# Differential attention on one core: the next key tile's steps moved between a head's score groups, and three of its four rows turned at the head's end

## The chip, the cores and the metric

The kernel runs on one core of one Trainium2 chip. The time is the device time of one execution in microseconds (us), the median of three executions. Five engines run their own instruction streams and meet through semaphores: TensorE (PE in the profile, its weight loads PEld), VectorE (DVE), ScalarE (ACT), GpSimd (POOL) and SyncE (SP, which only issues the loads).

## What is computed

A small transformer of two blocks, 512 positions of width 1024, in float32. The change is in one part of the second block, the differential attention, with 8 heads of two maps of 64 each:

```
k, v   = split(rms_norm(x, g_kv) @ w_kv)
q      = (h @ w_q), 8 heads x 2 maps x 64
logits = einsum('bqhmd,bkhmd->bhmqk', q, k) * 64**-0.5 + bias[h, dist]     (causal)
probs  = softmax(logits)
attn   = probs[:, :, 0] - lam * probs[:, :, 1]
o      = rms_norm(attn @ v, subln_g) * (1 - lambda_init)
mix    = o @ w_o
```

## The kernel before

Every tensor lies with its features (or keys) on the 128 partitions and the 512 positions along the free dimension. Every float32 product is made of three matmuls: each operand is split into a rounded high part (made by ACT, `..._hi`) and the rest (made by DVE or POOL, `..._lo`), and high x high, high x low and low x high are summed in a PSUM bank (`mm`, L755). Weights come in units of 8 blocks of 128x128: SP loads a unit (L715), ACT writes its high part (L732, tile WH), DVE its low part (L741, tile WL), always two units ahead.

There is no scheduler. Each engine's order is written out by hand in a function of its own (`pe_dif`, `act_dif`, `dve_dif`, `pool_dif`), all with the same loop over the heads h = 0..7, and a wait is put in where an event of another engine is needed. `plan_dif` lists in program order who sits in which PSUM bank and which temporary tile; a step that writes a bank waits until the bank's previous tenant has been read (`freed`, L384).

In a head, PE does these steps:

- **scores(h, i)** for the four rows of 128 queries, i = 0..3 (L2269): per map p three matmuls of 128*(i+1) keys into a bank of its own. The banks come from a ring of three (banks 2 to 4). DVE then adds the bias and finds the row maximum (L2544), ACT takes the exponential (L2411), and after two rows DVE's `combine` (L2554 to L2564) subtracts the two maps.
- **turn(h, i)** (L2282): the i+1 blocks of a row are transposed into a bank of a ring of two (banks 5 and 6; rows 0 and 1 share one). ACT copies the high part (L2418), DVE writes the low part (L2570), which frees the bank.
- **key(h + 1)** (L2252): the next head's key tile, eight steps k = 0..7 of three 512-column matmuls, read out by DVE at L2525.
- **value** (L2256): one half of a value tile, 48 matmuls of 256 columns, read out at L817 (ACT) and L826 (DVE).
- **values(h - 1)** (L2291): the product of the turned rows with v, in bank 7.
- **sums_of(h - 1)** (L2304) and **finish(h - 2)** (L2314): the sum of squares of a head's output (which DVE turns into an inverse root, L2583 and L880 to L892), and the spread of that root over the partitions, which ACT copies (L2434) and DVE multiplies in (L2596).

Key tiles, value halves, sums and spreads share a ring of two banks (0 and 1). The seats are handed out in the order of `plan_dif`; before, the key tile is seated ahead of the spread:

```
if h < 7:
    key(h + 1)
...
if h >= 2:
    finish(h - 2)
```

so a key tile follows a value half in its bank, and the spread follows the sums. `sums_of(h - 1)` stands at the end of head h on PE, and DVE reads its bank in the next head, after `scores`.

In head 7 there is no next key tile; steps of the output projection `w_o_2` (k, m) stand there instead, by the table `DIF_OUT`, in which each name is a place in the head and each pair is one step of three 512-column matmuls.

Of the kernel before, what the change touches and what calls it, by code (L numbers as in the profile page):

```python
# [48 lines left out]
def nope_q(h):  # L49
# [49 lines left out]


DIF_OUT = {
    "head 7, a": [(k, 0) for k in range(5)],
    "head 7, b": [(5, 0)],
    "turn": [(k, m) for k in range(3) for m in (1, 2, 3)],
    "values": [(k, m) for k in (3, 4) for m in (1, 2, 3)],
    "sums": [(5, 1), (5, 2)],
    "root": [(5, 3)] + [(6, m) for m in range(4)],
    "spread": [(k, 4) for k in range(7)],
# [163 lines left out]
class Net:  # L272
# [352 lines left out]
    def plan_dif(self):  # L625
        seat, bank = self.seat, self.bank
        self.ring = Ring(bank[0:6])
        self.plan_entry("dif")
        seat(self.tmp.next(), "t", "dif", "lam")
        seat(bank[7], "dif", "q", 6)  # L630
        seat(bank[6], "dif", "q", 7)
        pr, srg, ptr = Ring(bank[0:2]), Ring(bank[2:5]), Ring(bank[5:7])
        self.extra = [Slot(self.fd(4096, 512)), Slot(self.fd(4608, 512)), Slot(self.R2), Slot(self.acc[:, :])]
        own, self.tmp = self.tmp, Ring(self.tmps + self.extra)
        tmp = self.tmp

        def key(h):
            seat(pr.next(), "dif", "k", h)
            seat(tmp.next(), "t", "dif", "k", h)

        def value(c, p):
            seat(pr.next(), "dif", "v", c, p)

        def scores(h, i):
            for p in range(2):
                seat(srg.next(), "dif", "s", h, i, p)
                if p == 0 or i >= 2:
                    seat(tmp.next(), *self.dif_row(h, i, p))

        def turn(h, i):  # L650
            seat(ptr.next(), "dif", "t", h, i)

        def values(h):
            seat(bank[7], "dif", "pv", h)
            seat(tmp.next(), "t", "dif", "osq", "h", h)

        def sums_of(h):
            seat(pr.next(), "dif", "hs", h)

        def finish(h):  # L660
            seat(pr.next(), "dif", "hr", h)
            for x in "rt":
                seat(tmp.next(), "t", "dif", x, h)

        for h in range(8):
            seat(tmp.next(), "t", "dif", "q", h)
        key(0)
        value(0, 0)
        for h in range(8):
            scores(h, 0)  # L670
            if h:
                turn(h - 1, 2)
            scores(h, 1)
            scores(h, 2)
            if h:
                turn(h - 1, 3)
            if h < 7:
                key(h + 1)
            else:
                seat(bank[1], "dif", "o", 0)  # L680
                pr = Ring(bank[0:1])
            if h >= 2:
                finish(h - 2)
            scores(h, 3)
            if h:
                values(h - 1)
            if h < 7:
                value((h + 1) // 2, (h + 1) % 2)
            turn(h, 1)
            if h:  # L690
                sums_of(h - 1)
        turn(7, 2)
        turn(7, 3)
        finish(6)
        values(7)
        sums_of(7)
        finish(7)
        for m in range(1, 5):
            seat(bank[m + 1], "dif", "o", m)
        self.tmp = own  # L700
        for m in range(5, 8):
            seat(bank[m - 5], "dif", "o", m)
        for m in range(1, 8):
            seat(own.next(), "t", "dif", "osq", m)
# [1543 lines left out]
    def pe_dif(self, pe):  # L2248
        QZ, pt, xin = self.dif_qz, self.dif_pt, self.xin(0)

        def key(h):
            self.pe_tile(pe, ("dif", "k", h), "w_kv_2", h, KD, xin, (lambda k: ("xkv", k)) if h == 0 else None,  # L2252
                         {4: lambda: finish(h - 3)} if h >= 3 else None)

        def value(c, halves):
            self.pe_natural(pe, "dif", c, "w_kv_2", (8 + 2 * c, 9 + 2 * c), KD, xin, None, halves)  # L2256
# [17 lines left out]
        def turn(h, i):  # L2274
            b = self.dif_turned(h, i)
            pe.wait_ge(*self.at("probs", "dif", h, i))
            if i != 1:
                for w in self.freed("dif", "t", h, max(i, 1)):
                    pe.wait_ge(*w)
            for j in range(i + 1):  # L2280
                sl = slice(128 * j, 128 * j + 128)
                m = pe.transpose(b[:, sl], self.dif_s(h, i, 0)[:, sl], self.ident[:, :])  # L2282
            m.then_inc(*self.tick("pe_turn", ("pe", "dif", "t", h, i), ("free", *self.dif_row(h, i, 0))))
# [24 lines left out]
        def finish(h):  # L2308
            b, y = self.place["dif", "hr", h], self.small(("hy", h), 4)
            pe.wait_ge(*self.at("hy", h))  # L2310
            for w in self.freed("dif", "hr", h):
                pe.wait_ge(*w)
            for c in range(4):
                m = pe.matmul(b[:, 128 * c:128 * c + 128], y[:, c:c + 1].broadcast_to([P, P]), self.ident[:, :],  # L2314
                              start=True, stop=True)
            m.then_inc(*self.tick("pe_spread", ("pe", "dif", "hr", h)))
# [26 lines left out]
        for h in range(8):  # L2343
            scores(h, 0)
            if h:
                turn(h - 1, 2)
            scores(h, 1)
            scores(h, 2)
            if h:
                turn(h - 1, 3)  # L2350
            if h < 7:
                key(h + 1)
            else:
                out(DIF_OUT["head 7, a"])
                finish(5)
            scores(h, 3)
            if h:
                values(h - 1)
            if h < 7:
                value((h + 1) // 2, [(h + 1) % 2])  # L2360
            else:
                out(DIF_OUT["head 7, b"])
            turn(h, 0)
            turn(h, 1)
            if h:
                sums_of(h - 1)
        turn(7, 2)
        out(DIF_OUT["turn"])
        turn(7, 3)
        finish(6)  # L2370
        out(DIF_OUT["values"])
# [10 lines left out]
    def act_dif(self, act):  # L2382
# [79 lines left out]
        for h in range(8):  # L2462
            scores(h, 0)
            if h:
                turn(h - 1, 2)
            scores(h, 1)
            scores(h, 2)
            if h:
                turn(h - 1, 3)
            if h < 7:  # L2470
                key(h + 1)
            else:
                out(DIF_OUT["head 7, a"])
                finish(5)
                rounded(5)
            scores(h, 3)
            if h:
                values(h - 1)
            if h < 7:
                c = (h + 1) // 2  # L2480
                if h % 2:
                    self.hi_to(act, BLOCK["w_kv_2", KD - 1, 9 + 2 * c])
                value(c, [(h + 1) % 2])
                if h % 2 == 0:
                    self.hi_to(act, BLOCK["w_kv_2", KD - 1, h + 1])
            else:
                out(DIF_OUT["head 7, b"])
            turn(h, 0)
            turn(h, 1)
        turn(7, 2)  # L2490
        out(DIF_OUT["turn"])
        turn(7, 3)
        finish(6)
        out(DIF_OUT["values"])
# [9 lines left out]
    def dve_dif(self, dve):  # L2504
# [9 lines left out]
                *self.tick("q_in", ("q_in", h), ("free", *b)))  # L2514

        def key(h):
            if h % 2 == 0:
                self.lo_to(dve, BLOCK["w_kv_2", KD - 1, h])
            if h >= 3:
                finish(h - 3)  # L2520
            t, b = ("t", "dif", "k", h), ("dif", "k", h)
            dve.wait_ge(*self.at("pe", *b))
            for w in self.freed(*t):
                dve.wait_ge(*w)
            dve.tensor_tensor(self.place[t], self.place[b], R, ALU.mult).then_inc(  # L2525
                *self.tick("dif_kin", ("dif_kin", h), ("free", *b)))
# [106 lines left out]
        for h in range(8):  # L2633
            scores(h, 0)
            if h:
                turn(h - 1, 2)
            scores(h, 1)
            scores(h, 2)
            if h:
                turn(h - 1, 3)  # L2640
            if h >= 2:
                sums_of(h - 2)
            combine(h, 0)
            if h < 7:
                key(h + 1)
            else:
                out(DIF_OUT["head 7, a"])
                finish(5)
            scores(h, 3)
            combine(h, 2)  # L2650
            floor_of(h)
            if h < 7:
                c = (h + 1) // 2
                if h % 2:
                    self.lo_to(dve, BLOCK["w_kv_2", KD - 1, 9 + 2 * c])
                value(c, [(h + 1) % 2])
                if h % 2 == 0:
                    self.lo_to(dve, BLOCK["w_kv_2", KD - 1, h + 1])
            else:
                out(DIF_OUT["head 7, b"])  # L2660
            turn(h, 0)
            turn(h, 1)
        turn(7, 2)
        sums_of(6)
        out(DIF_OUT["turn"])
        turn(7, 3)
        finish(6)
        out(DIF_OUT["values"])
# [286 lines left out]
```

## Time and profile before

| | us |
|---|---|
| median of 3 executions | 2221.17 |
| lowest and highest | 2210.81, 2221.62 |
| the profiled execution, its own time | 2223.64 |
| its span, first to last instruction | 2221.8 |
| PE busy in it | 2032.3 (91%) |
| DVE, ACT, POOL busy | 1246.1, 814.0, 379.0 |
| mean granted TensorE clock | 0.947 of full speed |
| matmuls of the score groups (L2269), first to last start | 1512.9 to 1691.7 |

The part that the change touches is the stretch from about 1513 to 1745 us of the span, a tenth of it. The rest of the kernel is the same in both. In what follows M is the moment at which PE ends the value half of a head, the last long matmul run before the next head's first scores; times in head h are counted from the M that ends head h-1. The stretches of the windows below run from M to M, heads 0 to 6 in order, and the last from head 7's M to its values(6).

### The profile page before, as it was taken

The numbers are of one execution on the slowest core, as the hardware profiler recorded it, in microseconds if no ns is written. First come the engines' busy times: TensorE is split into PE (matmuls) and PEld (weight loads), VectorE is DVE, ScalarE is ACT, GpSimd is POOL, SyncE is SP. The second block draws the span as 40 slices with busy tenths as digits, with TensorE's granted clock in tenths as the row PEclk, the third lists the DMA queues.
The fourth block names the chain that finished last, engine by engine and source line by source line (L and its number), as shares of the span: only waits on it lengthen the run. The fifth ranks groups of instructions, "written<-read, shape, count | busy, mean of one in ns | idle before, by whom it ended". The sixth has DMA issues, their size and how long they took to land.

```text
span 2221.8 us, 25395 instructions
## 1 busy us (share of the span) xinstructions
PE 2032.3 (91%) x9756; PEld 1696.6 (76%) x9756; DVE 1246.1 (56%) x2013; ACT 814.0 (37%) x1307; POOL 379.0 (17%) x300
## 2 busy tenths in 40 slices
PE   7999999989788999999999998798889899999996
PEld 6888888767667777877888787676777778887875
DVE  6665664266665354457777425565555577774255
ACT  4233232243333332334444223334444444442232
POOL 3322321110222210121111011121001311110111
PEclk9999999989888999999999999798889999999997
DMA  4222222312101123322223332122111122232221
GB/s 166 81 81 86 79 83 86 96 57 86 38 29 37 61 97 103 113 67 86 95 95 105 104 96 68 54 84 81 57 39 49 66 85 95 95 105 104 96 68 46
DMA packets 53664, 178.91 MB, mean 81 GB/s; under 512 B 6151, under 2 KB 8711, under 8 KB 53544
## 3 DMA queue, kind: packets, MB, share of 16 engines
q1 hardware_dynamic: 53544, 177.29, 24.0%
q8 instruction: 78, 1.28, 0.2%
q14 instruction: 42, 0.34, 0.1%
HBM read 172.55 MB, written 4.72 MB: 80 GB/s over the span
## 4 chain that ended last, share of the span: by engine, by line
PE 59%; DVE 11%; ACT 4%; issue 3%; POOL 1%; DVEq 0%; ACTq 0%
PE pb L758 55%; DVE WL L741 2%; ACT WH L732 1%; DVE X L922 1%; PE pb L2269 1%; PE pb L855 1%; DVE T L1703 1%; PE pb L839 1%; DVE FR L956 1%; PE pb L1457 1%; ACT T L942 1%; DVE sm L1692 0%; PE pb L1889 0%; DVE T L916 0%; DVE FR L826 0%
## 5 line engine op out<-in xcount | busy, mean ns | idle before, releaser
L758 PE MATMUL pb<-FR,WH 128*128 128x512 f32 x4552 | 1457.6, 402 | 70.5 <-DVE FR L956 28.7
L758 PEld LDWEIGHTS pb<-FR,WH 128*128 128x128 f32 x4552 | 874.2, 194 | 266.5 <-issue 39.6
L758 PE MATMUL pb<-FR,WL 128*128 128x512 f32 x2276 | 906.8, 398 | 0.0
L741 DVE TENSOR_TENSOR WL<-stage,WH 128x1024 fp32r<-128x1024 f32 x311 | 408.7, 1333 | 517.3 <-ACT WH L732 516.3
L758 PEld LDWEIGHTS pb<-FR,WL 128*128 128x128 f32 x2276 | 441.4, 194 | 95.9
L732 ACT ACTIVATE WH<-stage 128x1024 fp32r<-128x1024 f32 x311 | 319.2, 1051 | 122.0 <-PE pb L758 109.1
L758 PE MATMUL pb<-WH,FR 128*128 128x256 f32 x832 | 154.7, 284 | 6.0 <-DVE T L1675 3.8
L758 PE MATMUL pb<-FR 128*128 128x256 f32 (+3 forms) x752 | 129.1, 325 | 13.5 <-DVE T L1265 12.2
L758 PEld LDWEIGHTS pb<-FR 128*128 128x128 f32 x752 | 117.6, 204 | 27.6 <-DVE T L1265 14.8
L758 PEld LDWEIGHTS pb<-WH,FR 128*128 128x128 f32 x832 | 131.4, 192 | 8.0 <-DVE T L1675 4.7
L948 POOL TENSOR_TENSOR acc<-acc,T 128x512 f32<-128x512 f32 x56 | 75.7, 1352 | 277.1 <-ACT T L942 276.6
L1040 POOL TENSOR_TENSOR acc<-acc,T 128x512 f32<-128x512 f32 x48 | 62.1, 1294 | 349.2 <-ACT T L1023 296.3
L758 PE MATMUL pb<-WL,FR 128*128 128x256 f32 x416 | 117.7, 283 | 0.0
L931 ACT ACTIVATE FR<-X,cols 128x512 fp32r<-128x512 f32 x64 | 45.4, 721 | 148.2 <-DVE X L922 148.2
L758 PEld LDWEIGHTS pb<-WL,FR 128*128 128x128 f32 x416 | 79.8, 192 | 0.1
L2101 POOL TENSOR_TENSOR FR<-FD,FR 128x512 fp32r<-128x512 f32 x26 | 34.2, 1316 | 242.2 <-ACT FR L2032 242.2
L1023 ACT ACTIVATE T<-pb 128x512 f32<-128x512 f32 x42 | 25.8, 614 | 126.7 <-PE pb L758 126.7
L1869 ACT ACTIVATE FD<-FD,cols 128x512 f32<-128x512 f32 x42 | 30.2, 724 | 101.5 <-DVE FD L2062 57.5
L922 DVE TENSOR_TENSOR X<-X,T 128x512 f32<-128x512 f32 x64 | 58.9, 922 | 0.2
L1357 POOL TENSOR_TENSOR FR<-T,FR 128x512 fp32r<-128x512 f32 (+3 forms) x32 | 28.0, 906 | 167.6 <-ACT FR L1193 167.6
L916 DVE SCALAR_TENSOR_TENSOR T<-FD,cols,pb 128x512 f32<-128x512 f32 x64 | 47.2, 738 | 14.6 <-PE pb L855 14.6
L817 ACT ACTIVATE FR<-pb,held 128x256 fp32r<-128x256 f32 x64 | 26.4, 474 | 76.3 <-PE pb L758 76.3
(223 smaller groups left out, 1669.7 us busy)
## 6 DMA issues: line engine op xcount, KB each, us to landing
stage<-in_ws SPq DMA_DIRECT2D x311, 512.0 KB, 3.5
X<-in_xT SPq DMA_DIRECT2D x8, 256.0 KB, 5.9
FD<-in_decay SPq DMA_DIRECT2D x8, 256.0 KB, 3.7
FD<-scr SPq DMA_DIRECT2D x1, 2048.0 KB, 10.0
out_dram<-X SPq DMA_DIRECT2D x8, 256.0 KB, 2.0
scr<-T SPq DMA_DIRECT2D x8, 160.0 KB, 1.8
scr<-FD SPq DMA_DIRECT2D x8, 160.0 KB, 1.9
FD<-in_rope_b SPq DMA_DIRECT2D x2, 512.0 KB, 3.4
```

The source lines that it names most:

```text
L732: act.activation(hi, src, ACT.Copy).then_inc(*self.tick("w_hi", ("w_hi", u)))
L741: dve.tensor_tensor(lo, src, hi.bitcast(F32), ALU.subtract).then_inc(*self.tick("w_lo", ("w_lo", u)))
L758: m = pe.matmul(out, l, r, start=first and i == 0, stop=last and i == n - 1)
L817: act.activation(dst(t)[0], src, ACT.Copy, scale=self.hold(y)[:, t:t + 1]).then_inc(*self.tick("v_hi", ("v_hi", s, h, t)))
L916: dve.scalar_tensor_tensor(out=t, in0=self.Y[k], scalar=self.col(name, base + k), in1=self.place["spread", s, "post"], op0=ALU.mult, op1=A ...
L922: dve.tensor_tensor(self.xt(k), self.xt(k), self.place["t", s, "z", k], ALU.add).then_inc(*self.tick("added", ("x", s, k), ("free", "t", s ...
L931: act.activation(self.xin(at)(0, k), self.xt(k), ACT.Copy, scale=self.col(name, base + k)).then_inc(*self.tick("xg_hi", ("xg_hi", s, g, k)))
L948: pool.tensor_tensor(self.acc[:, :], self.acc[:, :], self.place["t", s, "sq", k], ALU.add).then_inc(*self.tick("acc", ("acc", s, "x", k), ...
L1040: pool.tensor_tensor(self.acc[:, :], self.acc[:, :], self.place["t", s, "osq", m], ALU.add).then_inc(*self.tick("acc", ("acc", s, "y", m), ...
L1357: pool.tensor_tensor(S[:, 1280 + o:1280 + o + n], self.place["t", "ret", "s", h, j][:, 0:n], S[:, o:o + n].bitcast(F32), ALU.subtract).the ...
L1869: act.activation(self.place[o], self.place[u], ACT.Copy, scale=w).then_inc(*self.tick("tap", done))
L2101: pool.tensor_tensor(M[:, (NF + m) * 512:(NF + m) * 512 + 512], self.place[t], M[:, 512 * m:512 * m + 512].bitcast(F32), ALU.subtract).the ...
```

## The change

In a head, PE's steps were: scores 0, turn(h-1, 2), scores 1, scores 2, turn(h-1, 3), the key tile with the spread in it, scores 3, values, the value half, turn 0, turn 1, sums. Now they are: scores 0, turn(h-1, 3), key steps 0 and 1, scores 1, key steps 2 to 4, scores 2, key step 5, the spread, key steps 6 and 7, scores 3, values, the value half, turn 0, turn 1, turn 2, sums. ACT and DVE follow in their streams; DVE does the arithmetic of `sums_of(h - 2)` now between its row 3 and the bias of scores 1. `plan_dif` seats the spread ahead of the key tile. In head 7 the table spreads the first output steps over the same gaps. Cut to what matters:

```diff
 DIF_OUT = {
-    "head 7, a": [(k, 0) for k in range(5)],
-    "head 7, b": [(5, 0)],
+    "head 7, a": [(0, 0), (1, 0)],
+    "head 7, b": [(2, 0), (3, 0)],
...
@@ plan_dif
         for h in range(8):
             scores(h, 0)
             if h:
-                turn(h - 1, 2)
+                turn(h - 1, 3)
             scores(h, 1)
             scores(h, 2)
-            if h:
-                turn(h - 1, 3)
-            if h < 7:
-                key(h + 1)
-            else:
+            if h == 7:
                 seat(bank[1], "dif", "o", 0)
                 pr = Ring(bank[0:1])
             if h >= 2:
                 finish(h - 2)
+            if h < 7:
+                key(h + 1)
             scores(h, 3)
...
             turn(h, 1)
+            turn(h, 2)
             if h:
                 sums_of(h - 1)
-        turn(7, 2)
         turn(7, 3)
@@ pe_dif
         def key(h):
             self.pe_tile(pe, ("dif", "k", h), "w_kv_2", h, KD, xin, (lambda k: ("xkv", k)) if h == 0 else None,
-                         {4: lambda: finish(h - 3)} if h >= 3 else None)
+                         h and {1: lambda: scores(h - 1, 1), 4: lambda: scores(h - 1, 2),
+                                5: lambda: h >= 3 and finish(h - 3)})
...
             scores(h, 0)
             if h:
-                turn(h - 1, 2)
-            scores(h, 1)
-            scores(h, 2)
-            if h:
                 turn(h - 1, 3)
             if h < 7:
                 key(h + 1)
             else:
                 out(DIF_OUT["head 7, a"])
+                scores(h, 1)
+                out(DIF_OUT["head 7, b"])
+                scores(h, 2)
+                out(DIF_OUT["head 7, c"])
                 finish(5)
...
             turn(h, 0)
             turn(h, 1)
+            if h < 7:
+                turn(h, 2)
             if h:
                 sums_of(h - 1)
+        out(DIF_OUT["turn"])
         turn(7, 2)
-        out(DIF_OUT["turn"])
         turn(7, 3)
@@ act_dif
             if h:
-                turn(h - 1, 2)
+                turn(h - 1, 3)
             scores(h, 1)
             scores(h, 2)
-            if h:
-                turn(h - 1, 3)
...
             turn(h, 1)
+            if h < 7:
+                turn(h, 2)
@@ dve_dif
         def key(h):
+            if h >= 3:
+                finish(h - 3)
             if h % 2 == 0:
                 self.lo_to(dve, BLOCK["w_kv_2", KD - 1, h])
-            if h >= 3:
-                finish(h - 3)
...
             scores(h, 0)
             if h:
-                turn(h - 1, 2)
-            scores(h, 1)
-            scores(h, 2)
-            if h:
                 turn(h - 1, 3)
             if h >= 2:
                 sums_of(h - 2)
+            scores(h, 1)
             combine(h, 0)
+            scores(h, 2)
             if h < 7:
                 key(h + 1)
...
             turn(h, 1)
+            if h < 7:
+                turn(h, 2)
```

How this stands in the instruction streams, in head 4. First PE, from scores 0 (128 columns) on, before; FD and T are the tiles of the rows 2 and 3 that are turned (L2282):

```order
L2269 MATMUL pb<-FR 128x128 [waits s_biased,s_k_lo,s_q_lo]
L2269 MATMUL pb<-FR 128x128 x5
L2282 MATMUL pb<-ident,FD 128x128 [waits s_pt_lo,s_probs]
L2282 MATMUL pb<-ident,FD 128x128 x2
L2269 MATMUL pb<-FR 128x256 [waits s_biased]
L2269 MATMUL pb<-FR 128x256 x5
L2269 MATMUL pb<-FR 128x384 [waits s_biased]
L2269 MATMUL pb<-FR 128x384 x5
L2282 MATMUL pb<-ident,T 128x128 [waits s_pt_lo,s_probs]
L2282 MATMUL pb<-ident,T 128x128 x3
L758 MATMUL pb<-FR,WH 128x512 [waits s_w_lo,s_v_lo]
L758 MATMUL pb<-FR,WH 128x512
```

And in the changed kernel (the same lines are one number higher here), where FD has gone to the end of the head before:

```order
L2270 MATMUL pb<-FR 128x128 [waits s_biased,s_k_lo,s_q_lo]
L2270 MATMUL pb<-FR 128x128 x5
L2283 MATMUL pb<-ident,T 128x128 [waits s_pt_lo,s_probs]
L2283 MATMUL pb<-ident,T 128x128 x3
L758 MATMUL pb<-FR,WH 128x512 [waits s_w_lo,s_o_var]
L758 MATMUL pb<-FR,WH 128x512
L758 MATMUL pb<-FR,WL 128x512
L758 MATMUL pb<-FR,WH 128x512 x2
L758 MATMUL pb<-FR,WL 128x512
L2270 MATMUL pb<-FR 128x256 [waits s_biased]
L2270 MATMUL pb<-FR 128x256 x5
L758 MATMUL pb<-FR,WH 128x512 x2
```

The groups of 256 and 384 columns, scores 1 and 2, now have two and three key steps ahead of them; the first key matmul waited on `s_v_lo` (the value half's bank) and now waits on `s_o_var`, which DVE's first instruction of `sums_of` gives.

DVE in the same head before, from its row 2 (128x3x128) to `sums_of(2)` (the two groups between are the biases of scores 1 and 2):

```order
L2570 TENSOR_TENSOR FR<-pb,FR 128x3x128 [waits s_pt_hi]
L2544 ISA T,sm<-pb,FD 128x256 [waits s_pe_turn,s_pe_scores]
L2544 ISA sm 128x1
L2544 ISA T,sm<-pb,FD 128x256 [waits s_pe_scores]
L2544 ISA sm 128x1
L2544 ISA FD,sm<-pb,FD 128x384 [waits s_pe_turn,s_pe_scores]
L2544 ISA sm 128x1
L2544 ISA FD,sm<-pb,FD 128x384 [waits s_probs,s_pe_scores]
L2544 ISA sm 128x1
L2570 TENSOR_TENSOR FR<-pb,FR 128x4x128 [waits s_pt_hi]
L2583 SCALAR_TENSOR_TENSOR sm<-pb,sm 128x4 [waits s_pe_sums,s_o_var]
```

And in the changed kernel, from the end of the bias of scores 0:

```order
L2546 ISA T,sm<-pb,FD 128x128 [waits s_pe_scores]
L2546 ISA sm 128x1
L2572 TENSOR_TENSOR FR<-pb,FR 128x4x128 [waits s_pt_hi]
L2585 SCALAR_TENSOR_TENSOR sm<-pb,sm 128x4 [waits s_pe_sums,s_o_var]
L880 TENSOR_SCALAR sm<-sm 128x4 [waits s_o_var]
L882 SCALAR_TENSOR_TENSOR sm<-sm 128x4 [waits s_newton]
L884 TENSOR_TENSOR sm<-sm 128x4 [waits s_newton]
L886 SCALAR_TENSOR_TENSOR sm<-sm 128x4 [waits s_newton]
L889 SCALAR_TENSOR_TENSOR sm<-sm 128x4 [waits s_newton] x2
L892 SCALAR_TENSOR_TENSOR sm<-sm 128x4 [waits s_newton]
L2546 ISA T,sm<-pb,FD 128x256 [waits s_pe_turn,s_pe_scores]
L2546 ISA sm 128x1
```

Row 3 and the sums stand ahead of the bias of scores 1 now, and row 2 has gone ahead of the bias of scores 0.

## Rows read from the trace of the kernel before

**Rows 1.** The waits of PE, 1480 to 1725 us: in total, times, longest.
```profile
PE pb L2269 <- DVE sm L2544: 24.3, 16, 2.7
```
**Rows 2.** M to M: length, busy PE, PEld, DVE, ACT, POOL; clock, DMA share, GB/s.
```profile
1512.96:1531.12 18.16, 15.92 (x98) 13.28 (x99) 8.13 (x29) 6.27 (x19) 1.30 (x1) 0.91 0.17 59
1531.12:1556.03 24.91, 20.43 (x122) 17.06 (x120) 14.22 (x36) 11.86 (x29) 1.30 (x1) 0.86 0.16 49
1556.03:1579.53 23.50, 20.84 (x136) 17.68 (x135) 11.56 (x41) 9.26 (x26) 2.58 (x2) 0.93 0.10 39
1579.53:1605.01 25.48, 21.79 (x137) 18.60 (x135) 16.19 (x45) 13.08 (x30) 2.60 (x2) 0.87 0.17 47
1605.01:1629.14 24.13, 21.72 (x137) 18.60 (x136) 11.56 (x41) 9.33 (x27) 2.60 (x2) 0.86 0.10 39
1629.14:1653.93 24.79, 21.47 (x136) 18.20 (x134) 16.10 (x45) 13.02 (x30) 2.54 (x2) 0.86 0.15 52
1653.93:1677.19 23.26, 20.86 (x136) 17.94 (x135) 11.57 (x41) 9.29 (x26) 2.59 (x2) 0.93 0.09 36
1677.19:1693.02 15.83, 11.51 (x66) 8.83 (x64) 10.23 (x34) 8.03 (x22) 0.00 (x0) 0.78 0.09 33
```
**Rows 3.** Timeline of PE, head 3 (M = 1579.53): start, duration, idle before, releaser.
```profile
1583.50 0.63 PE L2269 MATMUL pb<-FR 64*128 64x256 f32 x6 [1.89 <-DVE sm L2544]
1585.93 1.33 PE L2269 MATMUL pb<-FR 64*128 64x384 f32 x6 [1.80 <-DVE sm L2544]
1587.19 1.11 PE L2282 MATMUL pb<-ident,T 128*128 128x128 f32 x4
1587.95 1.20 PE L758 MATMUL pb<-FR,WH 128*128 128x512 f32 x2
...
1591.73 0.63 PE L758 MATMUL pb<-FR,WH 128*128 128x512 f32 x2
...
1592.43 0.62 PE L758 MATMUL pb<-FR,WH 128*128 128x512 f32 x2
```
**Rows 4.** Timeline of DVE, head 3, from its share of the value half on.
```profile
1580.44 0.88 DVE L826 SCALAR_TENSOR_TENSOR FR<-pb,held,FR 128x256 fp32r<-128x256 f32 x2 [4.06 <-ACT FR L817]
1581.39 1.22 DVE L741 TENSOR_TENSOR WL<-stage,WH 128x1024 fp32r<-128x1024 f32 x1
1582.53 0.61 DVE L2570 TENSOR_TENSOR FR<-pb,FR 128x128 fp32r<-128x128 f32 x2
1583.06 0.28 DVE L2544 CUSTOM_DVE_ANT_0 T<-pb,FD 128x128 f32<-128x128 f32 x1
...
1584.88 0.56 DVE L2570 TENSOR_TENSOR FR<-pb,FR 128x384 fp32r<-128x384 f32 x1 [1.32 <-ACT FR L2418]
...
1590.16 0.69 DVE L2570 TENSOR_TENSOR FR<-pb,FR 128x512 fp32r<-128x512 f32 x1 [1.86 <-ACT FR L2418]
1590.77 0.15 DVE L2583 SCALAR_TENSOR_TENSOR sm<-pb,sm 128x4 f32<-128x4 f32 x1
...
1601.07 0.74 DVE L2564 SCALAR_TENSOR_TENSOR T<-T,sm 128x512 f32<-128x512 f32 x1
```
**Rows 5.** Timeline of ACT, head 3: the exponential of row 0, the copies of rows 2 and 3.
```profile
1583.60 0.40 ACT L2411 ACTIVATE T<-T,sm 128x128 f32<-128x128 f32 x1 [1.80 <-DVE sm L2544]
...
1584.38 0.47 ACT L2418 ACTIVATE FR<-pb 128x384 fp32r<-128x384 f32 x1
...
1589.55 0.57 ACT L2418 ACTIVATE FR<-pb 128x512 fp32r<-128x512 f32 x1
```
**Rows 6.** Timeline of DVE, head 4 (M = 1605.01), rows 0 and 1.
```profile
1606.71 0.61 DVE L2570 TENSOR_TENSOR FR<-pb,FR 128x128 fp32r<-128x128 f32 x2
```
**Rows 7.** Timeline of PE, head 0: the two waits.
```profile
1515.09 0.62 PE L2269 MATMUL pb<-FR 64*128 64x256 f32 x6 [1.66 <-DVE sm L2544]
1516.29 1.26 PE L2269 MATMUL pb<-FR 64*128 64x384 f32 x6 [0.58 <-DVE sm L2544]
```
**Rows 8.** Timeline of PE, head 7: values(6).
```profile
1693.02 2.10 PE L758 MATMUL pb<-FR 128*128 128x512 f32 x12 [0.95 <-DVE acc L2596]
```

More of the change, by code:

```diff
@@ L101 @@
 DIF_OUT = {
-    "head 7, a": [(k, 0) for k in range(5)],
-    "head 7, b": [(5, 0)],
-    "turn": [(k, m) for k in range(3) for m in (1, 2, 3)],
-    "values": [(k, m) for k in (3, 4) for m in (1, 2, 3)],
+    "head 7, a": [(0, 0), (1, 0)],
+    "head 7, b": [(2, 0), (3, 0)],
+    "head 7, c": [(4, 0)],
+    "head 7, d": [(5, 0)],
+    "turn": [(k, m) for k in range(2) for m in (1, 2, 3)],
+    "values": [(k, m) for k in (2, 3, 4) for m in (1, 2, 3)],
     "sums": [(5, 1), (5, 2)],
@@ L2361, in pe_dif @@
             else:
-                out(DIF_OUT["head 7, b"])
+                out(DIF_OUT["head 7, d"])
             turn(h, 0)
             turn(h, 1)
+            if h < 7:
+                turn(h, 2)
             if h:
                 sums_of(h - 1)
+        out(DIF_OUT["turn"])
         turn(7, 2)
-        out(DIF_OUT["turn"])
         turn(7, 3)
@@ L2472, in act_dif @@
             else:
-                out(DIF_OUT["head 7, a"])
+                out(DIF_OUT["head 7, c"])
                 finish(5)
@@ L2486, in act_dif @@
             else:
-                out(DIF_OUT["head 7, b"])
+                out(DIF_OUT["turn"])
             turn(h, 0)
             turn(h, 1)
+            if h < 7:
+                turn(h, 2)
         turn(7, 2)
-        out(DIF_OUT["turn"])
         turn(7, 3)
@@ L2646, in dve_dif @@
             else:
-                out(DIF_OUT["head 7, a"])
+                out(DIF_OUT["head 7, c"])
                 finish(5)
@@ L2659, in dve_dif @@
             else:
-                out(DIF_OUT["head 7, b"])
+                out(DIF_OUT["turn"])
             turn(h, 0)
             turn(h, 1)
+            if h < 7:
+                turn(h, 2)
+        sums_of(6)
         turn(7, 2)
-        sums_of(6)
-        out(DIF_OUT["turn"])
         turn(7, 3)
```

## The prediction

> **What bounds the kernel there.** PE is busy 91% of the span, so the first question is where it is not. I read the waits of PE over the attention first [rows 1]: the score groups wait for DVE 16 times, 24.3 us in all, twice in each head. Then the windows from M to M [rows 2]: a head takes 23.3 to 25.5 us, PE is busy 20.4 to 21.8 of them, and the granted clock is 0.86 to 0.93 of full speed; in heads 3 and 5 DVE has one more weight unit to make than in heads 2, 4 and 6, and they are the long ones. Then the timelines of one head. PE waits 1.89 us before scores 1 and 1.80 before scores 2 [rows 3], because the ring of score banks is three deep and DVE frees a bank only with the bias. DVE in turn is late because it has the value half, a weight unit and the turned rows in front of that bias [rows 4], and between them it waits for ACT's copies [rows 5]. Behind the waits the clock is at its low level: three key steps take from 1587.95 to 1591.73, 1.26 each, and the next one 0.70 [rows 3].
>
> So the attention costs more than its work in two ways, waits and the clock that falls behind them. The change means to put key steps into the two gaps. No arithmetic is added or taken away; what counts is which wait ends last in the new order.
>
> **The new start of a head, heads 2 to 6.** PE now does turn 2 at the end of the head before, so after scores 0 it comes to turn(h-1, 3) at about M + 2.1 (in head 3 before, the idle of 1.89 that ends at 1583.50 began at M + 2.1, after the same work) [rows 3]. Two waits follow.
>
> First, row 3 goes into the bank that rows 0 and 1 of the same head sit in, and that is free when DVE has written their low parts. In head 4 that is 1606.71 + 0.61, M + 2.3 [rows 6]; in head 3, with the weight unit ahead, 1582.53 + 0.61, M + 3.6 [rows 4]. With 0.1 for the semaphore PE goes on at M + 2.4 or M + 3.7, after 0.3 or 1.6 idle. The four blocks take 0.76 at the low clock [rows 3], 0.4 at the full one.
>
> Second, the key tile. Since the spread is now seated ahead of it, its bank's previous tenant is the sums of head h-2, which DVE reads with its first instruction of `sums_of`, and that stands behind the low part of row 3. The chain in an even head: DVE does row 2 (0.48, from 1584.88 to the next start) up to M + 2.75, and the bias of scores 0 (0.54 until ACT starts) [rows 4, 5], so ACT starts at M + 3.3; its exponentials take 0.78 (1583.60 to 1584.38), and only then comes its copy of row 3, 0.57 [rows 5], to M + 4.7; DVE's low part takes 0.61 and the read of the sums 0.15 [rows 4], to M + 5.45. PE starts the key tile at M + 5.55, after 2.7 idle. In heads 3 and 5 everything is 1.3 later, M + 6.85. Before, PE stood idle for 2.4 and 3.7 in these two kinds of head; now for 3.0 and 4.3. The gaps that the change fills are replaced by one that is larger.
>
> Behind it nothing else should wait: scores 1 needs the bias of scores 0, done before; scores 2 comes 2.1 us of key steps later, DVE's bias of scores 1 needs about 0.7 after its matmuls; scores 3 has three key steps and the spread ahead of it.
>
> The work from the start of the key tile to the next M was 17.06 in head 3 (1587.95 to 1605.01), of which the three slow steps were 3.78 where full clock gives 2.1, so 15.4 [rows 2, 3]. Scores 1 (0.6) and scores 2 (half of 1.33) come into it: 16.7 [rows 3]. Then the clock. Before, from the end of the second wait the rest of a head is scores 2, row 3 and the 15.4, 16.5; the wait ends at M + 5.1 or 6.4, which gives 21.6 and 22.9, and heads 2 to 6 took 23.50, 25.48, 24.13, 24.79 and 23.26 [rows 2]. The differences, 1.9, 2.6, 2.5, 1.9 and 1.7, are the low clock, 2.1 on average. The idle stretch is no shorter now, so I take 2.1 again. One more term in heads 3 and 5: ACT has a weight unit ahead of its copy of the spread there (its busy time is 13.1 in them against 9.3 [rows 2]), the spread itself comes later in the key tile, and values(h-1) needs the bank that DVE frees with that product. In head 7, also an odd one, this wait was 0.95 [rows 8]; I take 0.65, between nothing and that.
>
> An even head: 5.55 + 16.7 + 2.1 = 24.35. Heads 3 and 5: 6.85 + 16.7 + 2.1 + 0.65 = 26.3. Three and two of them make 125.65, against 121.16 before (1556.03 to 1677.19) [rows 2]: **+4.5**.
>
> **Head 1** has no sums of an older head, so its key tile can start behind row 3. It is one of the heads with a weight unit: row 3 at M + 3.7, key tile at M + 4.1, then 16.7 less the spread it doesn't have (eight blocks of 128 columns, 0.9 by the four of a row), plus 2.1: 22.0 against 24.91 [rows 2]: **-2.9**.
>
> **Head 0** turns nothing at its start. Its waits were 1.66 and 0.58 [rows 7]; two key steps (1.4) cover the first but for about 0.3, so 1.9 goes, and without the idle time the clock should stay: 0.09 of 18.16, 1.6 [rows 2]. **-3.5**.
>
> **Head 7.** Its output steps wait for no sums bank, but DVE now has row 3 and the eight small operations of the sums ahead of the bias of scores 1, and scores 2 waits for that; and values(6), which waited 0.95 before [rows 8], hangs on the same chain of ACT and DVE. I cost it at **0**, between -1 and +1. The output steps behind it are 42 as before, in another order; PE has nothing but them to wait with, and they cover the turns of rows 2 and 3 by six steps of 0.7 instead of nine.
>
> **Moved for nothing.** Turn 2 at the head's end needs `combine` of rows 2 and 3. Before, in head 3, DVE's product for row 2 stood just before that of row 3, which ended at 1601.07 + 0.74, 3.2 us ahead of M [rows 4]; in odd heads it will come about 2 us later. The cover is values and the value half, some 8 us of PE (the 15.4 less eight key steps, the spread and scores 3); if it is gone, each us late is one us of PE. The unit loads of SP are not moved past anything.
>
> **The sum** is 4.5 - 2.9 - 3.5 + 0 = -1.9. The profiled execution took 2223.64, which gives 2221.7; it lies 2.5 above the median of the runs, 2221.17, and so the median to expect is **2219**. A measurement of this kernel can tell about 0.5%, 11 us, from no change; its three runs alone spread over 10.8.
>
> The Trainium skill (Perfetto Trace Analysis, Optimization Strategy) says that the same gap repeating on the engine that should be saturated can mean too few banks for the next tile. The trace agrees: both old waits and both new ones are for a bank. Taken strictly it speaks against this change, which adds no bank: the 24.3 us would then only change their place, and the result would be 2221. The same page (Matmul Optimizations) says that TensorE scales its power with use and that matmuls should go out back to back in batches; by it a key tile cut into three pieces would lose a little, while here the pieces stand back to back with the scores.
>
> **Rivals.**
> *The gaps are covered (8%).* If the key tile's bank were free in time, all 24.3 us would go [rows 1] and with them the low clock behind, 2.1 in five heads and about 6.5 in heads 0, 1 and 7: 41 us, **2180**. For it speaks that 1.4 and 2.1 us of key steps match gaps of 1.9 and 1.8; against it the wait on `s_o_var` at the first key matmul.
> *The waits stay, but the clock does not fall (16%).* The idle time comes in one piece behind short work, and the key tile then runs without a break. If the clock stays up in heads 1 to 6, 2.1 us less in each: **2206**. Against it: before, it fell in every head, also in head 4 with 2.4 us idle [rows 2].
> *Slower (16%).* Turn 2 at the end of the head comes to the path. Its place is the last 0.3 us of a head: DVE's product for row 2 hangs on the spread, the weight unit and the key tile's readout ahead of the bias of scores 3. Once that chain is over about 2 us later than I walked it, PE stands there idle, the clock falls a second time, and the next head starts later on all engines. At 1.5 us of wait and 1.3 of clock in five heads that is 14 us: **2233**. Against it speaks the slack of 3.2 us before [rows 4].
> *The forecast (60%)*: the waits change places and heads 0 and 1 pay for heads 2 to 6, **2219**, and with the ends of its terms 2210 to 2228 (a clock loss of 1.0 to 3.2 per head, somewhat wider than the 1.7 to 2.6 seen, is 6 us each way over six heads, head 7 one, the 0.65 one, rounding one).
>
> **How the numbers follow.** The range runs from below the clock case to just under the slower case, 2203 to 2232; outside lie the covered case (8%) and part of the slower one. Faster by over 0.5% (below 2210) holds the first two rivals, 0.24; slower (above 2232) the third, 0.16; within is 0.60.
>
> **What the next profile should show.** The waits of score groups for DVE near nothing in heads 1 to 6 instead of 24.3; a new wait of the key tile's first matmul for the sums (L2583, now L2585), five times, about 2.7 each; waits of row 3's turn for the low part (L2570, now L2572), 0.3 and 1.6; heads 2 to 6 of 24.3 and 26.3 us, heads 0 and 1 shorter by 3 each. The forecast is wrong if the key tile starts before M + 4.5 in head 4, if the clock stays at 1.00 there, or if PE waits at the end of a head.

## The result, and the profile after

The changed kernel takes 2227.36 us, median of 19 executions (2224.45 to 2229.72), against 2223.02 us for the kernel before in as many (2210.81 to 2227.47). The ratio is 1.0021, 95% interval 1.0012 to 1.003: slower by 0.2%. That lies within the 0.5% that the prediction called no change and inside its range, but the forecast was 1.9 us down, and the median went 4.3 up. The profiled executions have spans, first to last instruction, of 2223.1 after and 2221.8 before.

The waits of PE over the attention in the changed kernel (engine, tile, line, who was waited for; us in total, times, longest):

```profile
PE pb L758 <- DVE sm L2585: 11.7, 5, 2.4
PE pb L2283 <- DVE FR L2572: 10.1, 7, 2.6
PE pb L758 <- DVE acc L2598: 5.2, 3, 3.7
...
PE pb L2270 <- DVE sm L2546: 1.3, 2, 0.7
```

The score groups' 24.3 us [rows 1] are down to 1.3, and two new waits make 21.8: the key tile's first matmul for the read of the sums (L2585), and row 3's turn for the low part of rows 0 and 1 (L2572). A third one, of values(h-1) for the spread's product (L2598), has grown from 0.9 to 5.2.

The windows from M to M in the changed kernel: heads 0 to 6, head 7 up to values(6), then to the end of the output matmuls, then to the first addition of the next stage (length, busy PE, PEld, DVE, ACT, POOL; clock, DMA share, GB/s):

```profile
1510.94:1525.77 14.83, 14.76 (x98) 12.03 (x99) 8.13 (x29) 6.28 (x19) 1.30 (x1) 1.00 0.22 72
1525.77:1546.07 20.30, 17.68 (x121) 14.65 (x119) 12.67 (x35) 11.85 (x28) 1.30 (x1) 1.00 0.17 52
1546.07:1570.49 24.42, 21.18 (x137) 17.52 (x135) 12.65 (x43) 9.13 (x26) 2.55 (x2) 0.93 0.14 44
1570.49:1597.47 26.98, 22.08 (x136) 18.15 (x135) 15.52 (x45) 12.95 (x30) 2.84 (x2) 0.87 0.12 40
1597.47:1621.54 24.07, 21.19 (x137) 17.53 (x135) 11.95 (x42) 9.13 (x26) 2.56 (x2) 0.93 0.12 44
1621.54:1648.59 27.05, 22.15 (x137) 18.23 (x135) 15.53 (x45) 12.96 (x30) 2.84 (x2) 0.87 0.12 40
1648.59:1672.65 24.06, 21.18 (x136) 17.43 (x135) 11.95 (x42) 9.14 (x26) 2.54 (x2) 0.93 0.12 44
1672.65:1689.12 16.47, 9.61 (x65) 7.28 (x64) 10.27 (x34) 7.90 (x22) 0.00 (x0) 0.98 0.08 33
1689.12:1741.92 52.80, 52.03 (x244) 43.83 (x244) 18.14 (x38) 20.96 (x36) 12.12 (x9) 0.94 0.22 75
1741.92:1748.81 6.89, 3.86 (x25) 3.39 (x23) 2.05 (x10) 1.08 (x2) 0.00 (x0) 0.82 0.10 39
```

The last two stretches in the kernel before:

```profile
1693.02:1743.21 50.19, 49.41 (x243) 41.41 (x244) 18.08 (x38) 20.91 (x36) 12.15 (x9) 1.00 0.25 79
1743.21:1749.40 6.19, 3.16 (x25) 2.79 (x23) 2.06 (x10) 1.08 (x2) 0.00 (x0) 0.93 0.13 52
```

Set beside [rows 2]: head 0 is 3.3 us shorter, head 1 4.6, heads 2 to 6 are 5.4 longer (126.58 against 121.16), head 7 up to values(6) 0.6 longer. Up to that point the changed kernel is 1.9 us ahead. Then it loses 2.6 in the output matmuls, at a clock of 0.94 where it was 1.00, and 0.7 in the norm behind. The whole attention, from the first M to that addition, takes 237.87 against 236.44: 1.4 us more.

PE in head 4 of the changed kernel (M = 1597.47; start, duration, idle before and who ended it):

```profile
1598.85 0.55 PE L2270 MATMUL pb<-FR 64*128 64x128 f32 x6
1599.94 0.63 PE L2283 MATMUL pb<-ident,T 128*128 128x128 f32 x4 [0.54 <-DVE FR L2572]
1602.91 1.13 PE L758 MATMUL pb<-FR,WH 128*128 128x512 f32 x2 [2.35 <-DVE sm L2585]
1605.68 0.95 PE L2270 MATMUL pb<-FR 64*128 64x256 f32 x6
```

And DVE at the same place:

```profile
1600.17 0.28 DVE L2546 CUSTOM_DVE_ANT_0 T<-pb,FD 128x128 f32<-128x128 f32 x1
...
1602.10 0.69 DVE L2572 TENSOR_TENSOR FR<-pb,FR 128x512 fp32r<-128x512 f32 x1 [1.43 <-ACT FR L2421]
1602.70 0.15 DVE L2585 SCALAR_TENSOR_TENSOR sm<-pb,sm 128x4 f32<-128x4 f32 x1
```

PE starts row 3 at M + 2.47 and the key tile at M + 5.44. DVE stands idle for 1.43 us, waiting for ACT's copy of row 3, while the small operation that PE waits for is ready to run and stands behind it.

In head 7 (M = 1672.65) the long wait is at values(6). ACT, DVE and PE in the changed kernel:

```profile
1686.02 1.04 ACT L732 ACTIVATE WH<-stage 128x1024 fp32r<-128x1024 f32 x1
1686.96 0.57 ACT L2437 ACTIVATE R<-pb 128x512 f32<-128x512 f32 x1
...
1687.09 1.22 DVE L741 TENSOR_TENSOR WL<-stage,WH 128x1024 fp32r<-128x1024 f32 x1 [2.32 <-ACT WH L732]
1688.23 0.74 DVE L2598 SCALAR_TENSOR_TENSOR acc<-pb,keep,R 128x512 f32<-128x512 f32 x1
...
1684.44 0.96 PE L2270 MATMUL pb<-FR 64*128 64x512 f32 x6 [0.61 <-DVE sm L2546]
1689.12 3.75 PE L758 MATMUL pb<-FR 128*128 128x512 f32 x12 [3.72 <-DVE acc L2598]
```

The copy and the product of the spread stand behind a weight unit on both engines. PE waits 3.72 us, against 0.95 before [rows 8], and its twelve matmul records behind the wait take 3.75 us instead of 2.10. The wait is longer for two reasons: PE gets there 2.1 us earlier in the head (M + 12.75, before M + 14.88), and the product comes 0.6 later. It comes later although its spread comes earlier from PE, because ACT reaches row 2's exponentials, which stand ahead of the unit and the copy, only at M + 12.2, where it reached them at M + 8.8. First the changed kernel, and below the dots the one before, whose M is 1677.19:

```profile
1682.61 0.17 DVE L2556 RECIPROCAL sm<-sm 128x2 f32<-128x2 f32 x1 [1.16 <-ACT T L2414]
1684.81 0.62 ACT L2414 ACTIVATE FD<-FD,sm 128x384 f32<-128x384 f32 x1 [2.22 <-DVE sm L2546]
...
1685.99 0.62 ACT L2411 ACTIVATE FD<-FD,sm 128x384 f32<-128x384 f32 x1 [1.09 <-DVE sm L2544]
```

In the changed order DVE does `combine` of rows 0 and 1 (L2556 on) ahead of the bias of scores 2, and waits 1.16 us there for ACT. That this order is what makes row 2 late is a reading of the trace; no run changes it alone.

### The profile page after: what moved, and what is told of

It reads as the page before. It is cut to its first block, busy times and chain, and to the rows that moved or that the text cites. A ratio compares the mean times of both kernels' runs of the same rounds, so it can differ in the third digit from the quotient of the medians.

```text
span 2223.1 us, 25395 instructions
## 1 busy us (share of the span) xinstructions
PE 2031.5 (91%) x9756; PEld 1692.8 (76%) x9756; DVE 1247.2 (56%) x2013; ACT 813.3 (37%) x1307; POOL 377.9 (17%) x300
## 3 DMA queue, kind: packets, MB, share of 16 engines
q1 hardware_dynamic: 53544, 177.29, 23.7%
## 4 chain that ended last, share of the span: by engine, by line
PE 60%; DVE 10%; ACT 4%; issue 3%; POOL 1%; DVEq 0%; ACTq 0%
PE pb L758 56%; DVE WL L741 2%; ACT WH L732 1%; PE pb L855 1%; DVE X L922 1%; DVE T L1703 1%; PE pb L839 1%; PE pb L2270 1%; PE pb L1457 1%; DVE FR L956 1%; DVE sm L1692 0%; ACT T L942 0%; PE pb L1889 0%; DVE T L916 0%; PE pb L843 0%
## 5 line engine op out<-in xcount | busy, mean ns | idle before, releaser
L741 DVE TENSOR_TENSOR WL<-stage,WH 128x1024 fp32r<-128x1024 f32 x311 | 408.7, 1333 | 524.1 <-ACT WH L732 523.4
L758 PE MATMUL pb<-FR 128*128 128x256 f32 (+3 forms) x752 | 130.1, 326 | 17.4 <-DVE T L1265 12.2
```

Of the source, the lines that this page charges most:

```text
L741: dve.tensor_tensor(lo, src, hi.bitcast(F32), ALU.subtract).then_inc(*self.tick("w_lo", ("w_lo", u)))
L758: m = pe.matmul(out, l, r, start=first and i == 0, stop=last and i == n - 1)
```

## The experiments

All times are medians of 6 to 12 executions, taken beside the kernel before, which was at 2224.05, 2224.11 and 2221.75 us in the three sets (the first four runs, the next four, the last four). So a difference of 2 us between runs of two sets says little. "Attention" is the length from the first M to the first addition of the next stage in the profile, 236.4 us before and 237.9 after.

**The changed kernel again** (`again`), unedited.

> The changed kernel itself, as the mark for the three others. In its first profile the attention, from the first scores to the first addition of the next stage, takes 237.9 us against 236.4 before, +1.4, while the medians differ by 4.3. If the clock's phase in the stages outside makes the rest, the time here is 2 to 6 us above before, and the attention again about 238 in its profile. If the attention itself makes all of it, its stretch is 240 or more in this profile.

2227.05 us, ratio 1.0018 (1.0002 to 1.0034), attention 238.0 us. Every head is within 0.05 us of the first profile: the new waits are not a matter of one execution. The attention does not make all of the difference. From its end to the end of the span both profiles of the changed kernel need 474.2 to 474.3 us and that of the kernel before 472.4, in code that is the same. Over all the profiles here that code took 469.7 to 474.5 us, and the unchanged code ahead of the attention 1502.7 to 1516.1.

**The key tile seated ahead of the spread** (`keyseat`), in the plan alone:

```diff
+            if h < 7:
+                key(h + 1)
             if h >= 2:
                 finish(h - 2)
-            if h < 7:
-                key(h + 1)
             scores(h, 3)
```

> Changed kernel, with the key tile seated ahead of the spread as before, so that it follows the value half in its bank and not the sums. Bank theory (the waits of 2.35 us for the read of the sums in heads 2 to 6 eat the gain): these five waits, 11.7 us, go, the low clock behind them goes or shortens, and the kernel is 12 to 20 us faster than the changed one, 2207 to 2215. Rival (DVE is late anyway, and the idle time only moves to scores 1 or scores 2, which wait for a bias that stands behind row 3 and the sums): 3 to 6 us faster, with new waits of the score groups of 1 to 2 us a head.

2209.64 us, ratio 0.9941 (0.9921 to 0.996), 17.4 below the changed kernel; attention 222.5, 15.5 shorter. The waits of its PE:

```profile
PE pb L2283 <- DVE FR L2572: 10.1, 7, 2.6
PE pb L758 <- DVE T L2598: 6.2, 5, 1.4
```

The wait for L2585 is not there any more, and no score group waits more than in the changed kernel. A part comes back elsewhere: values(h-1) of heads 2 to 6 now waits 6.2 us for the spread's product, where it waited 1.4, and the 3.7 in head 7 stay. Heads 2 to 6 take 21.5 to 23.7 us. The bank theory holds, with its size.

**The sums' arithmetic in DVE's idle time** (`sumsfirst`), ahead of row 3's low part:

```diff
             scores(h, 0)
+            if h >= 2:
+                sums_of(h - 2)
             if h:
                 turn(h - 1, 3)
-            if h >= 2:
-                sums_of(h - 2)
             scores(h, 1)
```

> Changed kernel, with DVE's eight small operations of the sums moved ahead of the low part of row 3, into the 1.4 us in which DVE waits for ACT's copy. Bank theory: the bank is free at about M + 3.5 instead of M + 5.4 in heads 2, 4 and 6, the key tile's wait falls from 2.35 to about 0.5, and scores 1 and 2 wait no more than now; 10 to 16 us faster than the changed kernel. Rival (DVE is the bound of a head's start): the gain comes back as waits elsewhere, under 4 us.

2205.07 us, ratio 0.9931 (0.9909 to 0.9953), 22.0 below the changed kernel, more than the 10 to 16 expected; attention 219.1, 18.9 shorter. The rest of the 22 lies in unchanged code.

```profile
PE pb L758 <- DVE sm L2585: 1.2, 5, 0.2
```

11.7 us of waiting became 1.2, and the clock over heads 1 to 6 rose from 0.92 to 0.97. One edit of where eight operations of 0.2 us stand is worth 0.9% of the kernel. Of the single edits to the changed kernel it gained the most.

**Head 7 alone: the weight unit behind the spread's product** (`fin7`), on ACT and DVE:

```diff
-                out(DIF_OUT["head 7, c"])
                 finish(5)
+                out(DIF_OUT["head 7, c"])
```

> Changed kernel, in head 7 alone: ACT and DVE make the weight unit of the third output group after the product of the spread and not before it. Tail theory (values(6) waits 3.72 us for that product, which stands behind a weight unit on ACT and on DVE, and the clock falls behind the wait): the wait falls by about 2 us to 1.7, the matmuls behind it run at full clock, and the kernel is 2 to 5 us faster than the changed one. Rival (the output steps then wait for the later unit): under 1 us, and a wait of PE for L741 appears in the profile.

2221.36 us, ratio 0.9989 (0.9971 to 1.0008), 5.7 below the changed kernel; attention 235.3.

```profile
1687.01 3.08 PE L758 MATMUL pb<-FR 128*128 128x512 f32 x12 [2.10 <-DVE acc L2598]
```

The wait falls from 3.72 to 2.10 and the stretch from values(6) to the end of the output from 52.8 to 51.6. No wait for L741 appears in that stretch. Of the 5.7 us the attention's profile shows 2.7: values(6) starts 1.6 us earlier in the head, the output is 1.2 shorter, and the norm behind is no shorter (7.1, against 6.9 and 6.2 in the kernel before). The code behind the attention, which is unchanged, gives 1.5. Without this fault the changed kernel is no longer distinguishable from the one before.

**The key steps in the gaps alone** (`gapsonly`), on PE alone, on the kernel before:

```diff
-                         {4: lambda: finish(h - 3)} if h >= 3 else None)
+                         h and {1: lambda: scores(h - 1, 1),
+                                4: lambda: (scores(h - 1, 2), h >= 2 and turn(h - 2, 3)),
+                                5: lambda: h >= 3 and finish(h - 3)})
...
```

> The kernel before with one part of the change alone, and on PE alone: key steps 0 and 1 ahead of scores 1, 2 to 4 ahead of scores 2, in head 7 output steps in the same way; turn 2 stays behind scores 0, turn 3 behind scores 2, the other engines and all seats as before. Theory (the gaps were fillable; the other two parts, row 3 at the head's start and the key tile behind the sums, put two new waits in their place): the key tile's bank is free at M + 2, scores 1 and 2 come when their banks are free, nearly all of the 24.3 us and of the low clock go, heads of 20 to 21 us, 25 to 40 us faster than before, 2185 to 2198. Rival (DVE and ACT cannot keep a head of 20 us, since they have 16 and 13 us of work in the odd ones): odd heads stay above 23 us, 10 to 15 us faster than before.

2225.78 us, ratio 1.0015 (0.9997 to 1.0032): attention 237.1: nothing gained, and the theory fell with its numbers.

```profile
PE pb L2316 <- DVE sm L892: 23.1, 6, 3.9
PE pb L2271 <- DVE sm L2547: 3.0, 5, 1.3
```

The score groups wait 3.0 us instead of 24.3, and the spread in the key tile waits 23.1 for the last of the sums' operations. On DVE these stand behind row 3, and ACT copies row 3 only after the exponentials of three rows. So the two parts I had blamed, row 3 at the start and the seat, are not needed for the gain to vanish; the place of the sums on DVE is enough.

**Row 2 at the head's end alone** (`turnend`), on all engines, on the kernel before:

```diff
-                turn(h - 1, 2)
+                pass
...
             turn(h, 1)
+            if h < 7:
+                turn(h, 2)
```

> The kernel before with the other part alone: row 2 is turned at the head's own end, on all engines; the key tile stays behind scores 2 in one piece. Theory: the wait before scores 1 grows by about 0.5 (row 2's low part stands ahead of the bias of scores 0), the wait before scores 2 falls from 1.8 to about 0.6 as in head 0; 3 to 7 us faster than before. Rival (the ready row is late at the head's end): PE waits for L2564 there and the kernel is not faster.

2219.23 us, 4.9 below the kernel before, ratio 0.9989 (0.9974 to 1.0004), attention 232.3, 4.1 shorter than before.

```profile
1580.02 1.01 PE L2271 MATMUL pb<-FR 64*128 64x256 f32 x6 [2.50 <-DVE sm L2550]
1581.61 1.33 PE L2271 MATMUL pb<-FR 64*128 64x384 f32 x6 [0.58 <-DVE sm L2550]
```

In head 3 the first wait grew by 0.6 and the second fell by 1.2, as expected. The time lies in the forecast 3 to 7, but its interval does not exclude no change.

**Both new waits taken away** (`turnlate`): the two edits above (the seat, and the sums ahead of row 3), and row 3 turned behind key step 1 on PE:

```diff
-                         h and {1: lambda: scores(h - 1, 1), 4: lambda: scores(h - 1, 2),
+                         h and {1: lambda: (h >= 2 and turn(h - 2, 3), scores(h - 1, 1)), 4: lambda: scores(h - 1, 2),
...
```

> Changed kernel with both new waits taken away: the key tile seated ahead of the spread, the sums' arithmetic in DVE's idle time ahead of row 3, and row 3 turned behind key step 1 on PE. Bank theory: the 10.1 us of waits for L2572 fall to under 2 and the 11.7 us for the sums are gone; heads of 19.5 to 21 us; 35 us or more faster than the changed kernel, 2180 to 2195. Rival (values(h-1) then waits for the spread's product, which is late on ACT and DVE, 1 to 3 us in odd heads): 20 to 30 us faster only.

2206.03 us, ratio 0.9935 (0.991 to 0.9959), 21 below the changed kernel: the rival's number, and not the theory's 35.

```profile
PE pb L758 <- DVE T L2597: 5.9, 5, 2.2
PE pb L758 <- DVE acc L2597: 3.7, 1, 3.7
...
PE pb L2283 <- DVE FR L2571: 1.8, 4, 1.0
```

Row 3's waits went from 10.1 to 1.8, and the attention is 218.5, hardly shorter than with the sums moved alone (219.1). The largest wait left is that for the spread's product, 9.6 us.

**The sums ahead of row 3 and head 7's unit together** (`combo`) (the edits of sumsfirst and fin7).

> Changed kernel with the sums' arithmetic ahead of row 3 and, in head 7, the weight unit behind the spread's product. If the two terms are independent, their gains add: 22 and 5, about 2200; if the wait of values(6) was already shortened by the first, 1 to 3 below it.

2206.38 us, ratio 0.9929 (0.9902 to 0.9956), attention 217.8: 1.3 shorter than the first edit alone, which the times do not show. The gains do not add: the wait of values(6) was already down to 2.85 and goes to 1.3.

**The gaps and the sums** (`gapsums`), on the kernel before: gapsonly, and DVE's sums ahead of row 2.

```diff
             scores(h, 0)
+            if h >= 2:
+                sums_of(h - 2)
             if h:
                 turn(h - 1, 2)
...
-            if h >= 2:
-                sums_of(h - 2)
             combine(h, 0)
```

> The kernel before, with the key steps in the gaps on PE alone (as gapsonly) and DVE's arithmetic of the sums moved ahead of the low part of row 2, where DVE waits 1.3 us for ACT. In gapsonly the spread inside the key tile waited 23.1 us in six heads for the last of these operations. Theory (this order on DVE alone held gapsonly back): that wait goes, the low clock behind it too, heads of 20 to 21 us (odd ones 22 to 24), attention 210 to 218 us, 18 to 28 us faster than before. Rival (the score groups or values(h-1) wait instead): heads stay at 23 to 25 us, under 8 us faster.

2199.16 us, ratio 0.9894 (0.9872 to 0.9915), attention 215.4. The one edit on DVE turns gapsonly's nothing into 1.1%. PE's waits for L892 are gone, and the attention is 21.7 us shorter than gapsonly's. The profile is of the fastest execution, 2189.48 us; the 10 us that it is below the median lie mostly in the unchanged code (1502.7 ahead of the attention, 469.7 behind).

**The same with the odd heads' weight unit behind the spread** (`best1`), on ACT and DVE:

```diff
-            if h % 2 == 0:
-                self.hi_to(act, BLOCK["w_kv_2", KD - 1, h])
             if h >= 3:
                 finish(h - 3)
+            if h % 2 == 0:
+                self.hi_to(act, BLOCK["w_kv_2", KD - 1, h])
+            if h >= 3:
                 rounded(h - 3)
```

(DVE's `lo_to` in the same way, and in head 7 the output's unit on both.)

> gapsums, with the weight unit of the odd heads (and of head 7) made behind the copy and the product of the spread on ACT and DVE. Theory (values(h-1) waits for that product behind a weight unit, 1.4 to 2.2 us with the clock falling in heads 3 and 5 and 3.7 in head 7): these waits go, odd heads come to 20 to 21.5 us, 4 to 10 us faster than gapsums. Rival (the unit comes late for PE or delays the bias of scores 3): under 2 us.

2196.76 us, ratio 0.989 (0.9872 to 0.9908). That is 2.4 below the last one, not the 4 to 10 expected, and the times of the two overlap; the attention is 209.9 against 215.4. The waits for the spread's product are shorter but not gone: 5.5 us in heads 2 to 6 and 2.4 in head 7, where gapsums had 7.7 and 3.6. Heads 1 to 6, head 7 up to values(6), and the output:

```profile
1525.74:1649.28 123.54, 115.16 (x791) 97.07 (x789) 79.20 (x249) 65.16 (x166) 14.63 (x11) 1.00 0.16 52
1649.28:1662.04 12.76, 9.55 (x67) 7.24 (x64) 9.02 (x33) 7.91 (x22) 0.00 (x0) 1.00 0.13 41
1662.04:1713.37 51.33, 49.66 (x244) 41.44 (x245) 19.18 (x39) 20.78 (x36) 12.38 (x9) 1.00 0.25 78
```

The clock is 1.00 throughout, and the odd heads take 21.0 us where they took 25 before. It beats both kernels.

**turnlate with the same edit.** (`best2`)

> turnlate with the same weight unit behind the spread. Theory: as for best1, 4 to 10 us faster than turnlate, 2196 to 2202. Rival: under 2 us.

2200.16 us, ratio 0.9903 (0.9887 to 0.9919), 5.9 below turnlate, of which 2.4 may be the lower level of this set; attention 211.7, 6.8 shorter. From the other side it ends at nearly the same place.

**A shift in time** (`shift`): the changed kernel with idle products of the identity before head 0.

```diff
...
+        for n in range(8):
+            pe.matmul(self.place["dif", "s", 0, 0, 0][:, 0:128], self.ident[:, :],
+                      self.ident[:, :], start=True, stop=True)
```

> Changed kernel with eight idle products of 128 columns (a constant by itself, overwritten by scores 0 of head 0) at the attention's start, 0.9 us of PE. If the clock's phase in the stages decides a part of the difference (the next stage's start runs at the low clock for longer in both profiles of the changed kernel than in the four others), the time moves by something else than +0.9, between -3 and +4, and the stretch from the attention's end to the span's end is 472.5 and not 474.2. If it is the change itself, that stretch stays 474.2 and the time is 0.5 to 1.5 above the changed kernel.

2229.63 us, ratio 1.0033 (1.0023 to 1.0044), 2.6 above the changed kernel, which was measured in a set whose kernel before stood 2.3 higher. The eight products were sixteen matmuls and took 1.9 us, not 0.9, so the expected price was too low. Attention 241.0, 3.1 longer: 1.7 in head 0, where the products stand, and 1.6 in head 1:

```profile
1529.57:1551.46 21.89, 19.27 (x120) 15.69 (x119) 12.97 (x36) 11.85 (x28) 1.30 (x1) 0.92 0.16 49
```

Head 1 has the same wait of 2.62 us in both, and the clock is 1.00 in one and 0.92 in the other. So the same idle stretch can cost nothing more or 1.6 us; whether its moment or the added products ahead decide that, this run does not tell. The code behind the attention takes 474.4, not the 472.5 I had named, so the shift does not show where the 1.8 us in the unchanged code come from.

## Why the prediction was wrong

**The two new waits at a head's start**: right. Row 3 was forecast at M + 2.4 and M + 3.7 and started at M + 2.47 and M + 3.76; the key tile was forecast at M + 5.55 and M + 6.85 and started at M + 5.44 and M + 6.73 (heads 4 and 3). The wait for the sums was to be 2.7 and was 2.35. keyseat and sumsfirst show that it is this wait that eats the gain in the changed kernel.

**Heads 2 to 6**: right in sign, small in size. Even heads 24.1 to 24.4, forecast 24.35; heads 3 and 5 27.0, forecast 26.3. The 0.65 for values(h-1) is 0.72. What is off is the low clock, 2.1 assumed in each: with the start at M + 6.73, 16.7 of work and 0.72 of wait, 2.8 are left for it in head 3, and by the same sum 1.9 in head 4. +5.4 instead of +4.5.

**Head 1**: -4.6 instead of -2.9. Its start was right, but I charged 2.1 for the clock, and it stayed at 1.00. **Head 0**: -3.3, forecast -3.5.

Up to M of head 7 the sum was thus -2.5, forecast -1.9.

**Head 7 is the step that failed**: "I cost it at 0, between -1 and +1". It cost 0.6 up to values(6) and 2.6 in the output matmuls behind, 3.2 in all, and with it the sign of the attention. The prediction named the chain, the wait for the spread's product, and even its row [rows 8], but gave no sum for its 0. It did not put the wait beside PE's own work: the score groups come earlier now, so PE meets a product that is 0.6 later with 3.7 us of idle time and not 0.95. And it priced the head only up to the wait: the clock falls for matmuls behind it that ran at full clock before. The edit of head 7 alone takes 2.7 us back in the attention and 5.7 in the time.

How much a wait of this length costs behind it is less settled. In keyseat it is as long, 3.72 us, and the output takes 51.45 us there, 1.3 more than before and not 2.6:

```profile
1679.98 3.56 PE L758 MATMUL pb<-FR 128*128 128x512 f32 x12 [3.72 <-DVE acc L2598]
```

The norm behind the output is 0.7 longer as well (6.89 against 6.19). That is not shown to come from head 7: with the wait cut to 2.10 in fin7 the norm took 7.11.

**The rest**: 1.4 us of the attention are not the 4.3 of the medians. The unchanged code behind took 1.9 us more in the profile and that before 2.0 less. It moved by more between other kernels here (469.7 to 474.5 behind the attention, 1502.7 to 1516.1 ahead of it). That part stays open. The measured 2227.36 lies 8.4 above the forecast 2219; 1.9 of that is the kernel before itself, 2223.02 in 19 executions and 2221.17 in the three that the forecast had.

**The rivals.** "Slower" was to come from row 2 at the head's end; no run shows PE waiting there. "The gaps are covered" was thought to give 2180 and to fail by the seat. With seat, sums and row 3 all mended the time was 2206, and the next wait on the chain, up to 3.7 us for the spread's product, was the largest left. With that one shortened too it came to 2200 (best2), and from the other side to 2197 (best1); no run came near 2180. "The waits stay, but the clock does not fall" came true in head 1 (a wait of 2.62 us, clock 1.00) and not in heads 2 to 6 (0.87 to 0.93). The rule of the Trainium skill on repeating gaps (Perfetto Trace Analysis, Optimization Strategy), taken strictly as more banks or nothing, is not borne out: gapsums has the same banks and seats as the kernel before, and the score groups' waits went from 24.3 us to 3.0 by the order on PE and DVE alone.

## What to carry to other kernels

When one engine's waits are filled with its other work, look at what the other engines have in front of the event that this work needs: here a 0.15 us operation stood behind a wait for a copy, and moving it with the seven that follow it into an idle slot of its own engine was worth 22 us, while filling the gaps alone was worth nothing. Walk the last turn of a loop by itself, where the successor's work is something else, and price a wait by both of its ends, where the waiting engine now arrives and when the event now comes. A wait in front of long dense work can cost more than the delay it makes: in head 7 the delay was 0.6 us, and the matmuls behind, at a clock of 0.94 and not 1.00, took 2.6 more.

## What was not expected of the hardware

The same idle time of 2.62 us in head 1 left TensorE's clock at full speed in the changed kernel (granted clock 1.00) and brought it down in shift, with eight idle products ahead of head 0 (0.92 over the head, 1.6 us longer). The same 3.72 us ahead of values(6) made the output matmuls 2.6 us longer in the changed kernel and 1.3 in keyseat. In best1, with waits of up to 1.3 us in heads 1 to 6 and one of 2.4 ahead of values(6), the clock stayed at 1.00 from head 1 to the end of the output. So the price of one wait in clock was between nothing and about 2.6 us here, and no run isolates what decides it.
